# A Mamba-2 mixer whose x is made with tokens on partitions, convolved from copies shifted by tokens, with dt and D folded into the decay matrix

## The reference, cut to what matters

```
zxbcdt = u @ in_proj                        # (256, 2048) @ (2048, 10304)
z, xbc, dt_raw = split(zxbcdt)              # 4096, 4096 + 2*1024, 64
xbc = silu(causal_depthwise_conv(xbc, conv_w, conv_b))   # 4 taps, along tokens
xs, B, C = split(xbc)                       # 8 groups of 8 heads of 64; 128 states a group
dt = softplus(dt_raw + dt_bias); a = dt * A; cum = cumsum(a) in each chunk of 128 tokens
y_intra[i] = sum_j (C_i . B_j) * exp(cum_i - cum_j) * dt_j * x_j      # j <= i, same chunk
y_inter[i] = C_i . state * exp(cum_i);      state = sum_j B_j * exp(cum_end - cum_j) * dt_j * x_j
g = (y_intra + y_inter + D * xs) * silu(z)
out = group_rms_norm(g) * gate_norm_w @ out_proj
```

## Time and profile before

| what | value |
|---|---|
| median of 3 runs | 2521.77 us (2521.69 to 2521.81) |
| the profiled execution | 2523.18 us, its span 2521.2 us |
| TensorE (matmul) busy | 2506.2 us, 99% of the span |
| VectorE, ScalarE, GpSimd busy | 1822.3, 1247.9, 155.6 us |
| DMA | 474.10 MB, 188 GB/s over the span |

### The profile page before, as it was taken

One profiled execution on the slowest core, in us unless ns is written; L12 is line 12 of the kernel. 1 busy time (PEld: TensorE's weight loads), 2 busy tenths in 40 slices (PEclk: granted clock), 3 DMA queues, 4 the chain that ended last, 5 costly groups with the idle time before them and its releaser, 6 DMA issues.

```text
span 2521.2 us, 42149 instructions
## 1 busy us (share of the span) xinstructions
PE 2506.2 (99%) x15444; PEld 2238.8 (89%) x15444; DVE 1822.3 (72%) x2572; ACT 1247.9 (49%) x1631; POOL 155.6 (6%) x271
## 2 busy tenths in 40 slices
PE   8999999999999999999999999999999999999999
PEld 8999999999898888888888998998898888888887
DVE  6977877787876675766667876778866667576667
ACT  7555555554654444444444754455644444444444
POOL 2222112211100000000000000000000000000000
PEclk9999999999999999999999999999999999999999
DMA  7666556656566566666656555555566656666664
GB/s 216 212 199 199 175 184 192 206 166 196 172 190 193 183 197 189 191 191 190 192 183 198 194 176 176 179 173 168 184 189 188 192 183 198 190 191 192 190 192 151
DMA packets 267240, 474.10 MB, mean 188 GB/s; under 512 B 16673, under 2 KB 50066, under 8 KB 265618
## 3 DMA queue, kind: packets, MB, share of 16 engines
q1 hardware_dynamic: 264194, 457.53, 59.2%
q0 software_dynamic: 2624, 15.00, 1.7%
q10 hardware_dynamic: 336, 0.41, 0.0%
HBM read 470.70 MB, written 2.19 MB: 188 GB/s over the span
## 4 chain that ended last, share of the span: by engine, by line
PE 98%; DVE 1%; ACT 1%; DMA 0%; issue 0%; SPq 0%; ACTq 0%; DVEq 0%
PE ps L1615 23%; PE ps L1616 23%; PE ps L1617 23%; PE ps L1644 16%; PE ps L1646 9%; PE ps L1873 1%; PE ps L1751 0%; PE ps L1971 0%; DMA h<-x 0%; PE ps L1878 0%; PE ps L1810 0%; PE ps L1779 0%; PE ps L2001 0%; PE ps L1729 0%; PE ps L1735 0%
## 5 line engine op out<-in xcount | busy, mean ns | idle before, releaser
L993 DVE TENSOR_TENSOR whl<-raw,whl 128x1024 fp32r<-128x1024 f32 x856 | 1062.5, 1242 | 592.1 <-ACT whl L664 579.5
L664 ACT ACTIVATE whl<-raw 128x1024 fp32r<-128x1024 f32 x856 | 906.7, 1059 | 1086.8 <-PE ps L1617 735.9
L1644 PE MATMUL ps<-xhl,whl 128*128 128x512 f32 x1792 | 623.0, 391 | 0.0
L1646 PE MATMUL ps<-xhl,whl 128*128 128x256 f32 x1792 | 505.4, 282 | 0.0
L1615 PE MATMUL ps<-whl,bhl 128*128 128x512 f32 x1284 | 500.8, 390 | 0.0
L1616 PE MATMUL ps<-whl,bhl 128*128 128x512 f32 x1284 | 499.5, 389 | 0.0
L1617 PE MATMUL ps<-whl,bhl 128*128 128x512 f32 x1284 | 499.5, 389 | 0.0
L1615 PE MATMUL ps<-xhl,whl 128*128 128x256 f32 x1748 | 493.9, 283 | 0.0
L1616 PE MATMUL ps<-xhl,whl 128*128 128x256 f32 x1748 | 488.5, 279 | 0.0
L1617 PE MATMUL ps<-xhl,whl 128*128 128x256 f32 x1748 | 487.9, 279 | 0.0
L1644 PEld LDWEIGHTS ps<-xhl,whl 128*128 128x128 f32 x1792 | 336.4, 188 | 70.9
(11 more groups left out here) (268 smaller groups left out, 2084.6 us busy)
## 6 DMA issues: line engine op xcount, KB each, us to landing
raw<-mlp_w SPq DMA_DIRECT2D x512, 512.0 KB, 4.2
raw<-a_in_proj SPq DMA_DIRECT2D x161, 512.0 KB, 4.5
raw<-a_out_proj SPq DMA_DIRECT2D x64, 512.0 KB, 4.0
raw<-b_w_q SPq DMA_DIRECT2D x32, 512.0 KB, 4.0
raw<-w_k SPq DMA_DIRECT2D x32, 512.0 KB, 4.0
raw<-w_v SPq DMA_DIRECT2D x32, 512.0 KB, 3.6
raw<-b_out_proj SPq DMA_DIRECT2D x32, 512.0 KB, 3.7
cumb<-cum_scratch POOLq DMA_DIRECT2D x8, 1024.0 KB, 7.7
```

What stands on the lines that cost most here:

```text
L664: sc.activation(slot_of(s, lo)[0], raw_of(s), ACT.Copy).then_inc(hi_ready, 1)
L993: ve.tensor_tensor(out=low, in0=raw_of(s), in1=hi.bitcast(F32), op=ALU.subtract).then_inc(lo_ready, 1)
L1644: te.matmul(ps[:, f, :].rearrange("p (q n) -> p q n", q=2), wh[:, j, c], xboth[:, :, k, :], start=k == 0, stop=False, skip_group_check=True)
L1646: last = te.matmul(ps[:, f, 0:S], wl[:, j, c], xhi[:, k, :], start=False, stop=k == KT - 1, skip_group_check=True)
```

## The change

- `xs` becomes token-major (also in the first four slabs of group 0, `high_first`). ScalarE copies the two banks to `taken`, with tokens on partitions and a block of zeros before the first 128.
- A shift by k tokens is now a shift over partitions: GpSimd issues six DMAs inside SBUF for each group (128 - k and k partitions, for k = 1, 2, 3), to the buffers `later`, two of which are yg and zs.
- The convolution (`convolve_tokens`) multiplies by weights that vary along the free dimension, which GpSimd fetches broadcast to all partitions (`conv_weights`: 4 x 512 and 512 values on 128 partitions). It is cut in five pieces of 1, 2, 2, 2 and 1 instructions of 128x1024, at bc 0 and acc 0 to 3 (z 1, 2, 4 and 5 in groups 0 and 7). One SiLU of 128x1024 follows at acc 4 (z 6).
- The 8 transposes, the copies of xs, xd and yg = D * x go. dt is multiplied in with the masked C.B (16 instructions of 128x128 instead of 2 of 128x1024), at acc 5 (z 3). D comes in as `skip`, a diagonal of D for each head, which GpSimd makes for each group and adds to m (2 instructions of 128x1024).
- The product of B and C moves to acc 3 (z 1), exp in groups 0 and 7 to z 2, the exponents of group 7 to xs 4.
- The last combination is 4 instructions of 128x512.
- norm_post_mix is loaded after the last group (its buffer holds the convolution's weights before).

```diff
-    SPREAD = {True: ("z", 3), False: ("acc", 7)}
+    CB = {True: ("z", 1), False: ("acc", 3)}
+    XS_CONV = {True: (("bc", 0), ("z", 1), ("z", 2), ("z", 4), ("z", 5)),
+               False: (("bc", 0), ("acc", 0), ("acc", 1), ("acc", 2), ("acc", 3))}
+    XS_SILU = {True: ("z", 6), False: ("acc", 4)}
-    DECAY = {True: ("z", 4), False: ("acc", 3)}
-    INTRA = {True: ("z", 4), False: ("acc", 7)}
+    DECAY = {True: ("z", 2), False: ("acc", 3)}
+    INTRA = {True: ("z", 3), False: ("acc", 5)}
...
+            def conv_weights(g):
+                cols = bass.ds(g * BLK, BLK)
+                pool.dma_start(conv_w, w["a_conv_w"][0][:, cols].partition_broadcast(P)).then_inc(conv_w_in, 16)
+                pool.dma_start(conv_b[:, :], w["a_conv_b"][0, cols].partition_broadcast(P)).then_inc(conv_w_in, 16)
+
+            def shift(g):
+                pool.wait_ge(pre_ready, 3 * g + 2)
...
+                for k in range(1, TAPS):
+                    pool.dma_start(later[k][k:, :, :], taken[0:P - k, 1:, :]).then_inc(later_in[k], 16)
+                    pool.dma_start(later[k][0:k, :, :], taken[P - k:, 0:MT, :]).then_inc(later_in[k], 16)
...
+                if above(g):
+                    conv_weights(g)
...
+                g_.tensor_copy(gdt[:, :, :], dt[:, :, bass.ds(g * R, R)])
+                chain.mark(g_.tensor_copy(gskip[:, :], hd[:, 2, bass.ds(g * R, R)]))
+                chain.wait()
+                chain.mark(g_.tensor_tensor(out=skip[:, :, :], in0=ident[:, :].unsqueeze(1).to_broadcast([P, R, P]),
+                                            in1=column_bcast(gskip[:, :], P), op=ALU.mult))
                 g_.tensor_copy(gcum[:, :, :], cum[:, :, bass.ds(g * R, R)]).then_inc(gcum_ready, 1)
...
+                shift(g)
+                chain.wait()
+                for c in range(MT):
+                    pool.wait_ge(m_scaled, 2 * g + c + 1)
+                    g_.tensor_tensor(out=m[:, c, :, :], in0=m[:, c, :, :], in1=skip[:, :, :], op=ALU.add).then_inc(mt_ready, 1)
                 pool.wait_ge(xs_ready, g + 1)
...
+                if (unit, i) == XS_SILU[z_first]:
+                    act.wait_ge(xs_conv, g + 1)
+                    sc.activation(xs[:, :, :], xs[:, :, :], ACT.Silu).then_inc(xs_ready, 1)
...
+                if n == 0:
+                    dve.wait_ge(pre_ready, 3 * g + 2)
+                    dve.wait_ge(conv_w_in, 32 * (g + 1))
...
+                    chain.mark(ve.tensor_tensor(out=xs[:, :, :], in0=taken[:, 1:, :], in1=bcast(conv_w[:, TAPS - 1, :]), op=ALU.mult))
+                elif n < TAPS:
+                    dve.wait_ge(later_in[n], 32 * (g + 1))
+                    link(ve.tensor_tensor(out=later[n], in0=later[n], in1=bcast(conv_w[:, TAPS - 1 - n, :]), op=ALU.mult))
+                    chain.mark(ve.tensor_tensor(out=xs[:, :, :], in0=xs[:, :, :], in1=later[n], op=ALU.add))
+                else:
+                    chain.wait()
+                    ve.tensor_tensor(out=xs[:, :, :], in0=xs[:, :, :], in1=bcast(conv_b[:, :]), op=ALU.add).then_inc(xs_conv, 1)
...
-                        ve.tensor_tensor(out=m[:, c, :, :], in0=m[:, c, :, :],
-                                         in1=cbm[:, c, :].unsqueeze(1).to_broadcast([P, R, P]), op=ALU.mult)\
-                            .then_inc(mt_ready, 1)
+                        for r in range(R):
+                            last = ve.scalar_tensor_tensor(out=m[:, c, r, :], in0=m[:, c, r, :], scalar=gdt[:, c, r:r + 1],
+                                                           in1=cbm[:, c, :], op0=ALU.mult, op1=ALU.mult)
+                        last.then_inc(m_scaled, 1)
...
                 if unit == "xs":
-                    feature_major(s, i, (0, 1), x)
+                    token_major(s, i, 8, 0, x)
...
                     if not first:
                         pe.wait_ge(acc_added, 4 * added)
-                    pe.wait_ge(pool_ready, g + 1)
+                    pe.wait_ge(xs_ready, g + 1)
```

More of the change, by code:

```diff
@@ L331, in build @@
         zs = mb("zs", [P, 4, S])
+        later = (None,) + tuple(b[:, :, :].rearrange("p f s -> p (f s)").rearrange("p (t n) -> p t n", t=MT)
+                                for b in (yg, zs)) + (later3[:, :, :],)
         cumb_room = mem.enter_context(nc.sbuf_tensor("cumb", [P, 2 * 4 * S], F32R, align_bytes=UNIT))
@@ L528, in _ @@
             g_.memset(ones[:, :], 1.0)
+            chain.mark(g_.memset(taken[:, 0, :], 0.0))
             chain.mark(g_.memset(ident[:, :], 0.0))
@@ L624, in _ @@
             chain.leave(G - 1, 4)
+            pool.wait_ge(xs_conv, G)
+            pool.dma_start(postw[:, :], w["norm_post_mix"][0].partition_broadcast(P)).then_inc(postw_in, 16)
             sum_squares(G)
@@ L836, in mix_step @@
                     last.then_inc(ecb_ready, 1)
-                if (unit, i) == SPREAD[z_first]:
-                    act.wait_ge(spread_done, 2 * g + 1)
-                    for c in range(MT):
-                        last = sc.activation(xs[:, c, :], ps[:, c, :], ACT.Copy)
-                    last.then_inc(xs_ready, 1)
                 if (unit, i) == ("z", 7):
@@ L1302, in time_steps @@
                 link(ve.tensor_scalar(dt[:, :, :], dt[:, :, :], 0.0, None, ALU.max))
-                for half in range(2):
-                    rows = slice(half * PD, (half + 1) * PD)
-                    ve.tensor_copy(dcol[rows, :], hd[rows, 2, half::2])
                 dve.wait_ge(dt_e, 1)
@@ L1386, in mix_step @@
                     gate_factor(g)
-                if (unit, i) == (("z", 0) if first else ("z", 1) if z_first else ("xs", 4)):
+                if (unit, i) == (("z", 0) if first else ("xs", 4)):
                     dve.wait_ge(cumb_in, 16 * (g + 1))
@@ L1397, in mix_step @@
                     last.then_inc(seg_done, 1)
[L1398 to L1399 removed]
+                if (unit, i) == ("bc", 3):
+                    convolve(first, g)
+                if (unit, i) in XS_CONV[z_first]:
+                    convolve_tokens(first, g, XS_CONV[z_first].index((unit, i)))
                 if unit == "acc":
                     add_output(mix, g - 1, i, MIX_LAST_BANKS if is_last(g, G) else MIX_OUT_BANKS)
[L1402 to L1403 removed]
+                if (unit, i) == CB[z_first]:
+                    dve.wait_ge(cb_done, g + 1)
                     ve.tensor_copy(cbx[:, :], ps[:, 2, P:2 * P])
@@ L1723, in high_first @@
                 wh, wl = slot(s, 2)
-                tiles = [(f, j) for f in range(4) for j in range(2)]
-                outs = [ps[:, f // 2, f % 2 * S:(f % 2 + 1) * S] for f in range(4)]
-                cols = [slice(f * P, (f + 1) * P) for f in range(4)]
+                tiles = [(t, j) for j in range(2) for t in range(MT)]
+                cols = [slice(t * P, (t + 1) * P) for t in range(MT)]
                 pe.wait_ge(x_hi, i + 1)
-                for f, j in tiles:
-                    te.matmul(outs[f], wh[:, j, cols[f]], xhi[:, 2 * i + j, :], start=i + j == 0 and f % 2 == 0, stop=False,
-                              skip_group_check=True)
+                for t, j in tiles:
+                    te.matmul(ps[:, t, :], xhi[:, 2 * i + j, cols[t]], wh[:, j, :], start=i + j == 0, stop=False, skip_group_check=True)
                 for n in turns:
@@ L1733, in high_first @@
                 pe.wait_ge(lo_ready, s.n + 1)
-                for f, j in tiles:
-                    te.matmul(outs[f], wl[:, j, cols[f]], xhi[:, 2 * i + j, :], start=False, stop=False, skip_group_check=True)
+                for t, j in tiles:
+                    te.matmul(ps[:, t, :], xhi[:, 2 * i + j, cols[t]], wl[:, j, :], start=False, stop=False, skip_group_check=True)
                 pe.wait_ge(x_lo, i + 1)
-                for f, j in tiles:
-                    last = te.matmul(outs[f], wh[:, j, cols[f]], xlo[:, 2 * i + j, :], start=False, stop=False, skip_group_check=True)
+                for t, j in tiles:
+                    last = te.matmul(ps[:, t, :], xlo[:, 2 * i + j, cols[t]], wh[:, j, :], start=False, stop=False, skip_group_check=True)
                 last.then_inc(slab_used, 1)
```

137 lines of the change are left out of this document (63 added, 74 removed).

## The result

The changed kernel takes 2615.55 us (median of 4 runs, 2611.37 to 2620.17) against 2521.73 for the kernel before: 1.0372 times as long, 95% interval 1.0355 to 1.0390. The forecast was 2565, with a range to 2590. It got the sign right and a little under half of the size.

A forecast was written before the change was run, and what follows sets the result against it. TensorE, 99% busy, was taken to bound the kernel, with VectorE's lag in its densest stretch making it wait. Group 0 +15, six loop groups +21 and group 7 +7 gave +43 on 2521.8: 2565 us, range 2535 to 2590.

The forecast's parts named there:

- A loop group, step by step: Groups 1 to 6: VectorE's late splits make TensorE wait 1.0 at z 0, 4.2 at z 2; 1.7 saved, +3.5 each.
- What I cost at nothing: Shifts, weight and bias loads, and GpSimd's extra DMA issues: 2.9 MB a group taken as hidden, 0 us.
- Group 0: First group: late cumb, landing at 70.2, delays VectorE's chain; TensorE goes on at 100.4 against 84.95, +15.
- Group 1: Counted as a loop group; its weights and cumb issued some 20 us later, costing 0 to 5 us, taken as 0.
- Group 7: Last group: xs ready at 32.4, TensorE ends z 7 at 23.5 and waits 8.9; with 1.7 saved, +7.
- TensorE's savings: Each group: token-major xs slabs save 0.10 to 0.11 each (0.8), the 8 transposes 0.93; 1.7 a group, 14 us over 8.
- m's scaling: VectorE at acc 5 (z 3): 16 instructions at 0.27, 4.3 in all, ends 3.2 and 6.4, against 3.46 before.
- GpSimd's part: Adding the diagonal to m beside VectorE: contention adds 1.0 (0 to 1.5) to m and 0.6 to the split for z 2.
- Rival 2: Clock falls after 8 long TensorE waits, one slab each at half rate, 2.8 each: +22, 2587. Chance 0.13.
- Rival 3: Shifts of 127 partitions crowd one DMA engine; TensorE waits about 10 more a group: +80, 2645. Chance 0.08.
- The gentle lag: m at 0.20 an instruction, no contention: +0.8 a loop group, groups 0 and 7 give 12 and 4, 2543. Chance 0.13.
- the gain: VectorE's lag at z 2 and z 7 absorbed by slack, so the 14 us saved show: 2508. Chance 0.05.

The follow-up runs named there:

- run with small shifts: Changed kernel with the six shift DMAs carrying 16 of 512 columns and the convolution reading the unshifted copy: 2599.71 us, 1.0310 of the kernel before.
- the pieces alone: Kernel before plus seven VectorE products of 128x1024 at acc 0 to 3, ahead of add_output, old convolution kept: 2584.33 us, ratio 1.0247.
- another relief: Changed kernel with GpSimd adding only one column of D's diagonal to m: 2602.84 us, 1.0321 of the kernel before.
- Spreading the pieces: Changed kernel, loop convolution pieces at acc 0, 2, 4, 6, SiLU at acc 7, m's scaling at z 0: 2623.11 us; with shifts also cut, 2584.50.
- phase run: Changed kernel with the split slabs of xs 4 to 7 moved 32 bytes further in their slots, as v's are: 2620.23 us, 1.0397.
- best version: Changed kernel, pieces spread, shifts in three turns from group 1, xs phase moved, first convolution weights later, groups 0 and 7 reordered: 2562.59 us, 1.0167.

## Why the prediction was wrong

**The step that failed** is "A loop group, step by step". It counted VectorE's queue against one kind of deadline, the splits ("TensorE wants z 0 at ... 22.7, so it waits 1.0; and z 2 at ... 29.3, so it waits 4.2"), and not against acc 6, which needs the add_output of acc 3. Its own numbers held the answer: it had that add_output done at 21.7 (22.4 less the 0.7 of C.B's copies, which follow it), and acc 6 begins at 6 x 2.72 + 0.9 (C.B, moved to acc 3) = 17.2. The difference is 4.5. The run with small shifts, whose loads are hardly late (ScalarE waits for a_out_proj once, 3.8 us), has almost that in each of groups 2 to 6:

```profile
258.22 0.79 PE L1660 MATMUL ps<-whl,bhl 128*128 128x512 f32 x1 [4.79 <-DVE y L1119]
```

In the changed kernel late loads come on top: 5.50 in group 2, where VectorE idled 0.63 for the split behind the load of 11 us. Once TensorE stands there, the splits are in time: the 1.0 and 4.2 never came, and waits for a split are 4.5 in all six entries. With 2 us for the half clock, which the forecast's own sum left out, and some 1.2 saved, 4.5 becomes +5.3 a group. The run with small shifts measured 5.5 in groups 2 to 6, the changed kernel 7.0 on average (6.0, 6.1, 5.4, 7.6, 9.9), against +3.5 forecast. The kernel before with the pieces alone shows that this wait, with the half clock behind it, comes without shifts and without GpSimd's additions.

**The shifts, "What I cost at nothing".** Right in the kernel before, where they cost 0.0 alone and 0.5 beside the pieces; not quite in the changed one, where the run with small shifts is 16 us shorter (some 11 of that with a place: 4.7 in group 1, and 6.5 in groups 5 and 6 that another relief ends as well). The row that I took the rate from (cumb, a load from memory) does not stand for copies inside SBUF: the engines were full at 222 to 323 GB/s. What held is that the copies land in time: VectorE never waited for one in the loop. What I did not ask is what they do to the loads beside them: a load of a_out_proj took 11 us (the chain has one issued at 235.6) instead of 4. Spreading the pieces gains 15 us on top of small shifts (2599.7 to 2584.5) and nothing without them, so in the changed kernel each cause covers part of the other. Why the loads suffer more there (a_out_proj 5.6 in the median of all its loads, the third pair of shifts 10.4) than with the same shifts in the kernel before (4.7 and 8.8, and 4.9 and 8.7 beside the pieces) was not settled: the sources differ (taken against postw), and so do the loads in flight.

**Group 0**, +15 forecast, +24.7 measured at y. cumb landed at 77.7, not at 70.2: issued 5.3 later than I had it (67.8; TensorE had stood for 4.5 at the turn of dt, which the run with later convolution weights took away), and 9.9 under way instead of 7.7. The two instructions beside GpSimd's addition cost 2.0 each more, 4.0 that I had not counted. The rest of the chain stood: exponents 3.2, m 4.3, xs at z 7 for ScalarE. And the wait of 13.8 was followed by y at half clock, 3.7 us instead of 2.0.

**Group 1**, forecast as a loop group ("0 to 5 us; I take 0"), added 14.6: the wait at acc 6 was 8.4, the half clock behind it cost 2.6, and the rest wasn't followed up. With small shifts 4.7 of the 14.6 go (93.0 instead of 97.7), 2.4 of them from this wait, which is 5.9 there. **Group 7**: the wait for xs was 11.0 (8.9 forecast), the group +12.2 (7).

**TensorE's savings**: the 8 transposes, 0.93, went; the 0.10 an xs slab did not. The rows of acc do not stand for xs: 12 x 0.233 = 2.80, against 2.83 for the old form. The phase run shows the reason: where the operands lie in SBUF.

**m's scaling**: 0.27 an instruction and 4.3 in all, as forecast from two rows. GpSimd's part was mis-sized: its two additions took 8.6 to 8.75 us and not 2 to 3 each, and the two splits beside them 2.3 each instead of 1.25 + 0.6. In groups 2 to 4 that didn't reach the end of the group: without the diagonal their steps are the same. The likely reason, not tested, is that the wait at acc 6 gives VectorE its lead back.

**The rivals.** Rival 2, the clock, was true as a mechanism: behind each wait at acc 6, 5.2 to 8.4 us long, 6 to 13 matmuls ran at 0.50, which cost 1.4 to 2.8 us and 2.0 on average (2.8 assumed), some 12 in all. The Trainium skill ("TensorE: Matmul & The Clock Gate", HAM oscillation) expects a fall at such waits, and the trace agrees: 0.50 in the window behind the wait. It was an addition to the main cause and not the cause itself: it comes behind a wait. Rival 3 (one engine carries 127 partitions) was false: the 127 partitions landed after 6.4 us, where one engine alone would have taken 21 by the prediction's estimate. The Trainium skill ("DMA: Bandwidth & Descriptors", Why a DMA increments its semaphore by 16) excepts some of GpSimd's copies from its divisor rule, and these behave like the exception. The gentle lag and the gain were far off.

The sum, by the table: 24.7 + 14.6 + 35.0 + 12.2 + 1.8 = 88.3, against 15 + 3.5 + 17.5 + 7 = 43.

## What to carry to other kernels

An engine that is "three slabs behind at most" has more than one deadline: list every semaphore that the bound engine waits for from it, above all those that free a bank, and set each against the queue, in program order. Here, by the prediction's own count, VectorE was 4.5 us late for the bank and 1.0 late for the first split. Work that hides by its mean (72% busy) is hidden only in the place where it is put, and the cheapest test of it is to add just that work to the kernel before; taking causes away one at a time misleads where one covers the other. The best version here, with pieces spread, shifts in turns and the edges reordered, takes back 53 of 94 us, and the old feature-major form stays ahead.
